# Another token block goes first through the final sums of a mixture-of-experts layer

## The chip, the cores and the metric

The kernel runs on one core of one Trainium2 chip. The metric is the device time of one execution in microseconds (us). Three executions of the kernel before took 1310.18, 1311.14 and 1313.49 us; their median is 1311.14 us.

The profile's short names are PE (TensorE, matrix multiplication), PEld (its weight loads), DVE (VectorE), ACT (ScalarE), POOL (GpSimd) and SP (SyncE, which here only issues DMAs). L473 is line 473 of the kernel before. In the changed kernel the same code stands one to eight lines lower.

## The reference

The layer takes 512 tokens of 1024 numbers. A mixing part gives the residual stream `x`; a mixture of 32 experts, of which each token uses four, is added to it; and a last norm is taken of every token:

```python
    x = x + jnp.concatenate([dn_out, pool_out], axis=-1) @ w_out[l]
    x = x + _moe(_rmsnorm(x, ffn_norm_w[l]), w_router[l], b_router[l],
                 w_gate_up[l], b_gate_up[l], w_down[l], b_down[l])
return _rmsnorm(x, final_norm_w)
```

Here `_rmsnorm(x, w)` is `x * rsqrt(mean(x*x) + 1e-6) * w` over the 1024 numbers of a token. The change touches only the last addition and the last norm.

## The kernel before

The kernel has one instruction list for each engine, written out by hand, and semaphores between them. Nothing reorders the lists, so the order of the code is the order of the work on each engine, and DMAs that SP issues go into one queue in the order of issue.

By far the longest part is a loop over blocks of 32 token assignments of one expert. PE multiplies with weights that SP streams into a ring of buffers; ACT scales the block's result (L851) and POOL writes it to DRAM with an indirect DMA (L604). POOL computes the row numbers of the next block (L600) only when its last indirect DMA has landed, and ACT waits for those row numbers before it writes the result for POOL. The results of all experts but the last one go to `pair_rows`, four rows for each token. The last expert's blocks are added in DRAM straight to `x1_rows`, which holds the residual stream.

After the loop come the final sums. The 512 tokens are four blocks of 128 (`TB` is 4), numbered 0 to 3:

- SP loads the four pair rows of each token, 2 MB for each block (L467), as soon as the other experts' results are in DRAM. It loads the norm's weights (L470), and when the last indirect DMA has landed, the residual rows, 512 KB for each block (L473). Each set is issued in the order 0, 1, 2, 3.
- DVE adds the four pair rows of blocks 0, 1 and 2 (L1421, three additions a block), and then the residual rows to them (L1424).
- PE does both for block 3: sixteen matmuls with an identity matrix add its pair rows in PSUM (L1998), and four more add its residual rows (L2002). The sum stays in PSUM as `summed_last`. These wait for `y_in[3]` and `x_in[3]`, the semaphores of block 3's loads.
- For each block ACT squares the sum and adds up over a token (L871, with a read of the accumulator), then takes a root (L873).
- For each block DVE takes the reciprocal of that root (L1428) and scales the block by it and by the norm's weights (L1429). SP stores the block when it is scaled (L476).

Four semaphores tie this together: `fin_sum` counts DVE's residual sums, `side_ps` tells that PE's sum is complete, `fin_rt` counts ACT's roots, and `fin_o` counts DVE's scaled blocks. In the kernel before, ACT, the scaling and the stores all take the blocks in the order 0, 1, 2, 3, and DVE finishes its three residual sums ahead of its first scaling.

Of the kernel before, what the change touches and what calls it, by code (L numbers as in the profile page):

```python
# [16 lines left out]
ALU, ACT, AX = mybir.AluOpType, mybir.ActivationFunctionType, mybir.AxisListType  # L17
# [4 lines left out]
TB = T // P  # L22
# [31 lines left out]
def moe_block(nc, x, attn_norm_w, w_in, conv_w, a_log, dt_bias, dn_norm_w, pool_w, pool_scale, w_out,  # L54
# [3 lines left out]
    with ctx:  # L58
        def sb(name, shape, dt=F32):
            return ctx.enter_context(nc.sbuf_tensor(name, shape, dt))  # L60

        def sem(name):
            return ctx.enter_context(nc.semaphore(name))
# [44 lines left out]
        xs = ring[:, X0 * UNIT:HOMES * UNIT].rearrange("p (b d) -> p b d", b=TB)  # L108
# [43 lines left out]
        sm = sb("sm", [P, 48])  # L152
# [15 lines left out]
        fnw = shared[:, 0:D]  # L168
# [52 lines left out]
        summed_last = ps[:, 4:6, :].rearrange("p a b -> p (a b)")  # L221
# [22 lines left out]
        def bc(v, n, at):  # L244

            return v.unsqueeze(at).to_broadcast([*v.shape[:at], n, *v.shape[at:]])
# [3 lines left out]
        par_in, wba_in, bc_in, pool_router_in, fnw_in, wout_in, braw_in = [sem(n) for n in (  # L250
            "par_in", "wba_in", "bc_in", "pool_router_in", "fnw_in", "wout_in", "braw_in")]
# [32 lines left out]
        fin_sum, fin_sq, fin_rt, fin_o, stored, act_step = [sem(n) for n in (  # L284
            "fin_sum", "fin_sq", "fin_rt", "fin_o", "stored", "act_step")]
# [5 lines left out]
        def chain(eng, s, start=0):  # L291

            n = [0]

            def link(ins):
                n[0] += 1
                ins.then_inc(s, 1)
                eng.wait_ge(s, start + n[0])
            link.n = n
            return link  # L300
# [11 lines left out]
        def slot_of(j, u):  # L312

            return (NU * j + u) % RING, (NU * j + u) // RING
# [6 lines left out]
        x1_quarters = x1_rows.rearrange("t (q c) -> (t q) c", q=Q)  # L321
        zeros = cat[:, 2048:2048 + D]
        pairs_in = ring[:, 4 * UNIT:12 * UNIT].rearrange("p (b c) -> p b c", b=TB)
        assert all(not 4 <= slot_of(E - 1, u)[0] < 12 for u in range(NU))

        halves = [slice(0, D // 2), slice(D // 2, D)]
# [26 lines left out]
        def _(sp):  # L353
# [109 lines left out]

            sp.wait_ge(scattered, others * 16)
            sp.wait_ge(late_out, 2 * 16)
            for b in range(TB):
                sp.dma_start(pairs_in[:, b], y_pairs[b * P:(b + 1) * P, :]).then_inc(y_in[b], 16)  # L467
            blocks = sp.value_load(tab[0:1, E:E + 1], min_val=E, max_val=MAXB)
            sp.wait_ge(w_used, blocks * NU)
            sp.dma_start(fnw, final_norm_w.rearrange("(a n) -> a n", a=1).to_broadcast([P, D])).then_inc(fnw_in, 16)  # L470
            sp.wait_ge(scattered, sp.value_load(looped[0:1, 2:3], min_val=E - 2, max_val=MAXB) * 16)
            for b in range(TB):
                sp.dma_start(xs[:, b, :], x1_rows[b * P:(b + 1) * P, :]).then_inc(x_in[b], 16)  # L473
            for b in range(TB):
                sp.wait_ge(fin_o, b + 1)
                sp.dma_start(out[0, b * P:(b + 1) * P, :], xs[:, b, :]).then_inc(stored, 16)  # L476
            sp.wait_ge(stored, 16 * (TB + 2))

# [158 lines left out]
        def _(act):  # L637
            A = nc.scalar.activation
            link = chain(act, act_step)
# [223 lines left out]
            with act.Fori(first, blocks) as g:  # L863
                activate(g)
            link(A(sm[:, 36:37], epsc[:, 0:1], ACT.Sqrt))
            for b in range(TB):
                if b < TB - 1:
                    act.wait_ge(fin_sum, b + 1)
                else:
                    act.wait_ge(side_ps, 4 + 2 + NU - NGU + 1)  # L870
                A(pairs_in[:, b, D:2 * D], xs[:, b, :] if b < TB - 1 else summed_last, ACT.Square, accum_out=sm[:, 28 + b:29 + b]).then_inc(fin_sq, 1)  # L871
                act.wait_ge(fin_sq, b + 1)
                A(sm[:, 32 + b:33 + b], sm[:, 28 + b:29 + b], ACT.Sqrt, scale=1.0 / D, bias=epsc[:, 0:1]).then_inc(fin_rt, 1)  # L873


# [1 line left out]
        def _(dve):  # L877
            V = nc.vector
            link = chain(dve, dve_step)

            def step(ins, s, count):

                ins.then_inc(s, 1)
                dve.wait_ge(s, count)
# [14 lines left out]
                                        op0=ALU.mult, op1=ALU.subtract))  # L899
# [23 lines left out]
            for k in range(KD):  # L923
                dve.wait_ge(xt_ps, k + 1)
                V.scalar_tensor_tensor(out=hT[:, k, :], in0=bank(k if k < KD - 1 else 2), scalar=pcol[:, NANW + k:NANW + k + 1],  # L925
                                       in1=rrow, op0=ALU.mult, op1=ALU.mult).then_inc(ht_ok, 1)
# [41 lines left out]
            def chunked(v):  # L968
# [21 lines left out]
                                        in1=bc(gt[:, 4, 0:2], NCH, 1), op0=ALU.mult, op1=ALU.mult), g_ok, 1)  # L990
# [296 lines left out]
            def swiglu_half(g, half, done, b, to=actT, told=actt_ok, by=1):  # L1287
# [4 lines left out]
                else:  # L1292
# [34 lines left out]
                                        op0=ALU.mult, op1=ALU.add))  # L1327
# [23 lines left out]
                                      op0=ALU.mult, op1=ALU.add))  # L1351
# [9 lines left out]
                                        op0=ALU.mult, op1=ALU.add))  # L1361
# [56 lines left out]
            for b in range(TB - 1):  # L1418
                dve.wait_ge(y_in[b], 16)
                for k in range(1, TOPK):  # L1420
                    link(V.tensor_tensor(pairs_in[:, b, 0:D], pairs_in[:, b, 0:D], pairs_in[:, b, k * D:(k + 1) * D], ALU.add))  # L1421
            for b in range(TB - 1):
                dve.wait_ge(x_in[b], 32)
                step(V.tensor_tensor(xs[:, b, :], xs[:, b, :], pairs_in[:, b, 0:D], ALU.add), fin_sum, b + 1)  # L1424
            dve.wait_ge(fnw_in, 32)
            for b in range(TB):
                dve.wait_ge(fin_rt, b + 1)
                link(V.reciprocal(sm[:, 44 + b:45 + b], sm[:, 32 + b:33 + b]))  # L1428
                V.scalar_tensor_tensor(out=xs[:, b, :], in0=xs[:, b, :] if b < TB - 1 else summed_last, scalar=sm[:, 44 + b:45 + b], in1=fnw, op0=ALU.mult,  # L1429
                                       op1=ALU.mult).then_inc(fin_o, 1)  # L1430


        @block.tensor
# [596 lines left out]
```

## Time and profile before

| what | before |
|---|---|
| median of three executions | 1311.14 us |
| the profiled execution | 1310.26 us, of which the span from first to last instruction is 1308.5 us |
| PE busy | 1263.3 us, 97% of the span |
| DVE busy | 515.7 us, 39% |
| ACT busy | 190.9 us, 15% |
| POOL busy | 162.7 us, 12% |
| DMA | 455.73 MB, 348 GB/s over the span |
| from the last matmul of the expert loop to the span's end | 25.0 us (1283.55 to 1308.5) |

The profiled execution is one of the quicker ones: it lies 0.9 us under the median of the three. Times within it count from the first instruction. The shares are averages over the whole span, in which the expert loop takes nearly all; the change lies in the last 25 us, so those are to be read by themselves.

### The profile page before, as it was taken

Reading aid. Unit: us, or ns where it says so; the run is one execution under the profiler, and the core shown is the slowest. Engines: PE = TensorE matmul, PEld = TensorE weight load, DVE = VectorE, ACT = ScalarE, POOL = GpSimd, SP = SyncE. Lnnn points to the kernel's source line nnn. Section 1 sums busy time; section 2 is a strip of 40 time slices with the busy share of each in tenths; the row PEclk is TensorE's granted clock in tenths of the full one; section 3 lists DMA queues with packets and bytes.
Section 4 is the critical chain, followed back from the end, with each engine's and each line's share of the span. In section 5 each row is a group of like instructions: output and inputs, shape, how many; then the busy total and the mean of one; then the engine's idle time right before and its main releaser. Section 6 shows DMA issues by size and latency. Waiting matters only on the chain.

```text
span 1308.5 us, 52719 instructions
## 1 busy us (share of the span) xinstructions
PE 1263.3 (97%) x21836; PEld 744.7 (57%) x21837; DVE 515.7 (39%) x1734; ACT 190.9 (15%) x439; POOL 162.7 (12%) x267
## 2 busy tenths in 40 slices
PE   8999999999999999999999999999999999989885
PEld 4545655445565665665665665656656656645452
DVE  5554223347343343343343333333433433423237
ACT  3431123332000000100100010000000000000002
POOL 4100430122111011011011011011011010100111
PEclk9999999999999999999999999999999999999999
DMA  7453131509999999999999999999999999999997
GB/s 237 140 188 129 34 133 48 222 33 372 416 402 415 421 414 422 415 421 416 420 417 421 413 421 415 421 410 421 416 417 422 417 420 416 420 421 421 421 424 277
DMA packets 80504, 455.73 MB, mean 348 GB/s; under 512 B 11057, under 2 KB 23018, under 8 KB 30730
## 3 DMA queue, kind: packets, MB, share of 16 engines
q1 hardware_dynamic: 76400, 445.69, 83.6%
q0 software_dynamic: 3888, 8.40, 1.8%
q8 instruction: 86, 1.41, 0.4%
q14 instruction: 24, 0.20, 0.0%
q10 hardware_dynamic: 106, 0.04, 0.0%
HBM read 432.53 MB, written 23.27 MB: 348 GB/s over the span
## 4 chain that ended last, share of the span: by engine, by line
DMA 52%; PE 43%; DVE 2%; issue 1%; ACT 1%; SPq 0%; DVEq 0%; POOL 0%; POOLq 0%; ACTq 0%
DMA ring<-in_w_gate_up_dram 32%; DMA ring<-in_w_down_dram 18%; PE ps L1900 12%; PE ps L1476 11%; PE ps L1952 6%; PE ps L1496 4%; PE ps L1866 2%; PE ps L1537 2%; DMA x_rows_dram<-cat,rowi 1%; PE ps L1530 1%; PE ps L1932 1%; DMA ring<-x_rows_dram 0%; PE ps L1892 0%; DVE ring L1429 0%; PE ps L1622 0%
## 5 line engine op out<-in xcount | busy, mean ns | idle before, releaser
L1900 PE MATMUL ps<-ring,cat 128*32 128x256 f32 x9856 | 550.1, 380 | 5.0 <-DMA ring<-in_w_gate_up_dram 4.9
L1900 PEld LDWEIGHTS ps<-ring,cat 128*32 128x32 f32 x9856 | 303.4, 110 | 221.7 <-DMA ring<-in_w_gate_up_dram 7.4
L1952 PE MATMUL ps<-ring,cat 128*32 128x256 f32 x4800 | 278.0, 382 | 12.7 <-DMA ring<-in_w_down_dram 12.4
L1952 PEld LDWEIGHTS ps<-ring,cat 128*32 128x32 f32 x4800 | 143.0, 110 | 118.2 <-issue 10.9
L1476 PE MATMUL ps<-hbuf,ring 128*128 128x512 f32 x320 | 146.0, 601 | 1.7 <-DVE hbuf L925 1.7
L1270 DVE TENSOR_REDUCE wslot<-ps 128x2 f32<-128x6 f32 x75 | 12.4, 165 | 320.0 <-ACT cat L851 318.5
L604 POOL DMA_INDIRECT pair_rows_dram<-cat,rowi x73 | 72.8, 997 | 436.9 <-ACT cat L851 436.9
L843 ACT ACTIVATE cat<-cat 128x128 f32<-128x128 f32 x154 | 47.6, 309 | 521.0 <-DVE cat L1294 521.0
L1866 PE MATMUL ps<-hbuf,cat 128*32 128x256 bf16 x2432 | 104.9, 273 | 1.1 <-DVE cat L1394 1.1
L1476 PEld LDWEIGHTS ps<-hbuf,ring 128*128 128x128 f32 x320 | 58.2, 190 | 67.2 <-issue 65.6
L1294 DVE TENSOR_SCALAR cat<-ps 128x128 f32<-128x128 f32 x154 | 44.8, 291 | 127.6 <-PE ps L1900 127.5
L851 ACT ACTIVATE cat<-ps,wslot 128x256 f32<-128x256 f32 x75 | 35.6, 474 | 369.7 <-PE ps L1952 363.5
L1866 PE MATMUL ps<-aux,cat 128*32 128x256 bf16 x1216 | 87.0, 273 | 0.0
L1866 PEld LDWEIGHTS ps<-hbuf,cat 128*32 128x32 bf16 x2432 | 66.6, 97 | 17.0 <-DVE cat L1394 1.6
L600 POOL TENSOR_TENSOR rowi<-rowj,qcol 128x1 int32<-128x1 int32 x75 | 15.7, 209 | 419.5 <-DMA pair_rows_dram<-cat,rowi 391.5
L1389 DVE COPY selu<-E 96x32 bf16 x75 | 13.3, 177 | 124.4 <-issue 124.4
L1496 PE MATMUL ps<-ring,cat 128*128 128x512 f32 x128 | 58.5, 600 | 2.3 <-DVE ring L1185 1.4
L1394 DVE TENSOR_TENSOR cat<-iotaf,rank 128x512 bf16 x75 | 51.9, 692 | 12.0 <-DVE gie L1390 12.0
L1302 DVE STREAM_TRANSPOSE cat<-cat 128x128 f32<-128x128 f32 x154 | 48.0, 312 | 5.3
L1298 DVE SCALAR_TENSOR_TENSOR cat<-cat 128x128 f32<-128x128 f32 x154 | 45.0, 292 | 5.3
L1301 DVE TENSOR_TENSOR cat<-cat 128x128 f32<-128x128 f32 x154 | 45.0, 292 | 5.2
L1295 DVE TENSOR_SCALAR cat<-ps 128x128 f32<-128x128 f32 x154 | 43.2, 281 | 0.0
(363 smaller groups left out, 817.3 us busy)
## 6 DMA issues: line engine op xcount, KB each, us to landing
ring<-in_w_gate_up_dram SPq DMA_DIRECT2D x256, 1024.0 KB, 10.0
ring<-in_w_down_dram SPq DMA_DIRECT2D x128, 1024.0 KB, 9.9
ring<-in_w_in_dram SPq DMA_DIRECT2D x10, 1024.0 KB, 6.3
pair_rows_dram<-cat SPq DMA_DIRECT2D x4, 2048.0 KB, 11.0
ring<-pair_rows_dram SPq DMA_DIRECT2D x4, 2048.0 KB, 19.8
ring<-in_w_out_dram SPq DMA_DIRECT2D x1, 4096.0 KB, 14.1
ring<-in_x_dram SPq DMA_DIRECT2D x4, 512.0 KB, 5.0
x_rows_dram<-ring SPq DMA_DIRECT2D x2, 1024.0 KB, 11.0
```

The source lines that it names most:

```text
L604: G.indirect_dma_start(out=into, out_offset=bass.IndirectOffsetOnAxis(ap=rowi[:, 0:1], axis=0), in_=ys, in_offset=None, bounds_check=limit ...
L843: A(sg[:, half], gc[:, half], ACT.Sigmoid, scale=ALPHA).then_inc(sg_ok, 1)
L1294: V.tensor_scalar(chunked_half(gc[:, half]), in_order(ps[:, b, 0:P]), LIMIT, None, ALU.min).then_inc(gc_ok, 1)
L1298: step(V.scalar_tensor_tensor(out=uc[:, half], in0=uc[:, half], scalar=1.0, in1=gc[:, half], op0=ALU.add, op1=ALU.mult), uc_step, n * 2 + 2)
L1301: step(V.tensor_tensor(act_[:, half], uc[:, half], sg[:, half], ALU.mult), act_ok, n + 1)
L1302: V.transpose(to[:, half], act_[:, half]).then_inc(told, by)
L1394: step(V.tensor_tensor(hot[:, :, :, :], slots, mine, ALU.is_equal), hot_ok, count)
L1476: last = mm(bank(m % 2), win[:, piece % 3, k, m % 2 * P:(m % 2 + 1) * P], hT[:, k, :], start=k == 0, stop=k == KD - 1)
L1496: last = mm(bank(n % 2), catT[:, k, b * P:(b + 1) * P], wout[:, k, 512 * half:512 * (half + 1)], start=i == 0, stop=i == KD - 1)
L1866: last = mm(ps[SLOTS * q:SLOTS * (q + 1), 2, 0:QD].rearrange("p (j i) -> p j i", i=SLOTS), hot[:, b, 0, :], rows, start=b == 0 and n == 0, ...
L1900: last = mm(ps[SLOTS * q:SLOTS * (q + 1), banks[half], 0:2 * P].rearrange("p (s m r) -> p s m r", s=2, m=2), x[:, SLOTS * u:SLOTS * (u + 1 ...
L1952: last = mm(ps[SLOTS * q:SLOTS * (q + 1), 1, 0:QD], actT[:, c // 4, SLOTS * (c % 4):SLOTS * (c % 4 + 1)], w[:, i, q * QD:(q + 1) * QD], st ...
```

## The change

A tuple `FINAL`, which is (3, 0, 1, 2), takes the place of the order 0, 1, 2, 3 in the pair loads, the residual loads, ACT's squares and roots, the scaling and the stores. DVE's list is also woven anew: after its residual sums of blocks 0 and 1 it scales one block each. Which engine sums which block, the number of instructions and all shapes stay as they are.

```diff
+        FINAL = (TB - 1, *range(TB - 1))
...
-            for b in range(TB):
+            for b in FINAL:
                 sp.dma_start(pairs_in[:, b], y_pairs[b * P:(b + 1) * P, :]).then_inc(y_in[b], 16)
...
-            for b in range(TB):
+            for b in FINAL:
                 sp.dma_start(xs[:, b, :], x1_rows[b * P:(b + 1) * P, :]).then_inc(x_in[b], 16)
-            for b in range(TB):
-                sp.wait_ge(fin_o, b + 1)
+            for n, b in enumerate(FINAL):
+                sp.wait_ge(fin_o, n + 1)
                 sp.dma_start(out[0, b * P:(b + 1) * P, :], xs[:, b, :]).then_inc(stored, 16)
...
-            for b in range(TB):
+            for n, b in enumerate(FINAL):
                 if b < TB - 1:
                     act.wait_ge(fin_sum, b + 1)
                 else:
                     act.wait_ge(side_ps, 4 + 2 + NU - NGU + 1)
                 A(pairs_in[:, b, D:2 * D], xs[:, b, :] if b < TB - 1 else summed_last, ACT.Square, accum_out=sm[:, 28 + b:29 + b]).then_inc(fin_sq, 1)
-                act.wait_ge(fin_sq, b + 1)
+                act.wait_ge(fin_sq, n + 1)
...
+            def scaled(n):
+
+                b = FINAL[n]
+                dve.wait_ge(fin_rt, n + 1)
+                link(V.reciprocal(sm[:, 44 + b:45 + b], sm[:, 32 + b:33 + b]))
+                V.scalar_tensor_tensor(out=xs[:, b, :], in0=xs[:, b, :] if b < TB - 1 else summed_last, scalar=sm[:, 44 + b:45 + b], in1=fnw, op0=ALU.mult,
+                                       op1=ALU.mult).then_inc(fin_o, 1)
+
+            dve.wait_ge(fnw_in, 32)
             for b in range(TB - 1):
                 dve.wait_ge(x_in[b], 32)
                 step(V.tensor_tensor(xs[:, b, :], xs[:, b, :], pairs_in[:, b, 0:D], ALU.add), fin_sum, b + 1)
-            dve.wait_ge(fnw_in, 32)
-            for b in range(TB):
-                dve.wait_ge(fin_rt, b + 1)
...
+                if b < TB - 2:
+                    scaled(b)
+            for n in range(TB - 2, TB):
+                scaled(n)
```

The end of DVE's list before, from the first residual sum on; `x_in0` to `x_in2` are the residual loads of blocks 0 to 2, and the row that reads `ps` scales block 3:

```order
L1424 TENSOR_TENSOR ring<-ring 128x1024 [waits x_in0,dve_step]
L1424 TENSOR_TENSOR ring<-ring 128x1024 [waits x_in1,fin_sum]
L1424 TENSOR_TENSOR ring<-ring 128x1024 [waits x_in2,fin_sum]
L1428 RECIPROCAL sm<-sm 128x1 [waits fin_rt,fnw_in,fin_sum]
L1429 SCALAR_TENSOR_TENSOR ring<-ring,sm 128x1024 [waits dve_step]
L1428 RECIPROCAL sm<-sm 128x1 [waits fin_rt]
L1429 SCALAR_TENSOR_TENSOR ring<-ring,sm 128x1024 [waits dve_step]
L1428 RECIPROCAL sm<-sm 128x1 [waits fin_rt]
L1429 SCALAR_TENSOR_TENSOR ring<-ring,sm 128x1024 [waits dve_step]
L1428 RECIPROCAL sm<-sm 128x1 [waits fin_rt]
L1429 SCALAR_TENSOR_TENSOR ring<-ps,sm,ring 128x1024 [waits dve_step]
```

The same end of DVE's list after:

```order
L1434 TENSOR_TENSOR ring<-ring 128x1024 [waits x_in0,fnw_in,dve_step]
L1427 RECIPROCAL sm<-sm 128x1 [waits fin_rt,fin_sum]
L1428 SCALAR_TENSOR_TENSOR ring<-ps,sm,ring 128x1024 [waits dve_step]
L1434 TENSOR_TENSOR ring<-ring 128x1024 [waits x_in1]
L1427 RECIPROCAL sm<-sm 128x1 [waits fin_rt,fin_sum]
L1428 SCALAR_TENSOR_TENSOR ring<-ring,sm 128x1024 [waits dve_step]
L1434 TENSOR_TENSOR ring<-ring 128x1024 [waits x_in2]
L1427 RECIPROCAL sm<-sm 128x1 [waits fin_rt,fin_sum]
L1428 SCALAR_TENSOR_TENSOR ring<-ring,sm 128x1024 [waits dve_step]
L1427 RECIPROCAL sm<-sm 128x1 [waits fin_rt]
L1428 SCALAR_TENSOR_TENSOR ring<-ring,sm 128x1024 [waits dve_step]
```

The scaling of block 3 moved from the end to the second place; it now stands ahead of the residual sums of blocks 1 and 2, and the last pair of rows scales block 2.

ACT's list before, its last five rows, from the root of block 1 on:

```order
L873 ACTIVATE sm<-sm,epsc 128x1 [waits fin_sq]
L871 ACTIVATE ring,sm<-ring 128x1024 [waits fin_sum]
L873 ACTIVATE sm<-sm,epsc 128x1 [waits fin_sq]
L871 ACTIVATE ring,sm<-ps 128x1024 [waits side_ps]
L873 ACTIVATE sm<-sm,epsc 128x1 [waits fin_sq]
```

ACT's list after, the five rows from the table load for the roots on:

```order
L866 ACT_TABLE_LOAD
L866 ACTIVATE sm<-epsc 128x1
L872 ACTIVATE ring,sm<-ps 128x1024 [waits side_ps,act_step]
L874 ACTIVATE sm<-sm,epsc 128x1 [waits fin_sq]
L872 ACTIVATE ring,sm<-ring 128x1024 [waits fin_sum]
```

The square of block 3, which reads PSUM and waits for PE, moved from the last place to the first, and block 0's square now stands behind it.

## Rows read from the trace of the kernel before

**Rows 1.** The page's chain that ended last: share of the span by engine.

```profile
DMA 52%; PE 43%; DVE 2%; issue 1%; ACT 1%; SPq 0%; DVEq 0%; POOL 0%; POOLq 0%; ACTq 0%
```

**Rows 2.** Chain that ended last, from 1272 us: start us, us, what.

```profile
1272.19 11.39 DMA x_rows_dram<-cat,rowi
...
1283.97 1.24 POOL rowi L600
...
1286.61 4.68 DMA x_rows_dram<-cat,rowi
...
1291.67 0.43 SPq L473
...
1292.15 6.27 DMA ring<-x_rows_dram
...
1298.52 1.24 DVE ring L1424
...
1299.78 0.17 DVE sm L1428
...
1299.98 1.28 DVE ring L1429
...
1304.16 1.28 DVE ring L1429
```

**Rows 3.** Timeline from 1279 us: start us, us, instructions in order, [idle before].

```profile
1279.92 3.63 PE L1952 MATMUL ps<-ring,cat 128*32 128x256 f32 x64
1280.19 11.26 DVE L1421 TENSOR_TENSOR ring<-ring 128x1024 f32<-128x1024 f32 x9
...
1288.97 8.70 PE L1998 MATMUL ps<-ring,cat 128*128 128x512 f32 x16 [5.42 <-DMA ring<-pair_rows_dram]
...
1290.80 0.34 PEld L1998 LDWEIGHTS ps<-ring,cat 128*128 128x128 f32 x1 [0.52 <-issue]
...
1291.66 0.34 PEld L1998 LDWEIGHTS ps<-ring,cat 128*128 128x128 f32 x1 [0.52 <-issue]
...
1294.08 0.19 PEld L1998 LDWEIGHTS ps<-ring,cat 128*128 128x128 f32 x1 [0.24 <-issue]
1294.50 0.19 PEld L1998 LDWEIGHTS ps<-ring,cat 128*128 128x128 f32 x1 [0.24 <-issue]
...
1299.72 1.98 PE L2002 MATMUL ps<-ring,cat 128*128 128x512 f32 x4 [2.05 <-DMA ring<-x_rows_dram]
...
1301.74 1.02 ACT L871 ACTIVATE ring<-ps 128x1024 f32<-128x1024 f32 x1 [0.48 <-PE ps L2002]
...
1302.89 0.29 ACT L873 ACTIVATE sm<-sm,epsc 128x1 f32<-128x1 f32 x1
```

**Rows 4.** From issue to landing, us: L467's four; its second; L473's four; its second; L476's.

```profile
DMA to landing us min/median/max: 12.7/19.8/26.7
...
ring<-pair_rows_dram SPq DMA_DIRECT2D x1, 2048.0 KB, 17.3
...
DMA to landing us min/median/max: 3.2/5.2/7.1
...
ring<-x_rows_dram SPq DMA_DIRECT2D x1, 512.0 KB, 4.2
...
DMA to landing us min/median/max: 2.6/2.6/2.7
```

**Rows 5.** POOL: L600 from 200 to 1250 us (ns min/median/max), then L604's last two.

```profile
L600 POOL TENSOR_TENSOR rowi<-rowj,qcol x73: 177/179/353, 329.8 to 1248.0; 128x1 int32<-128x1 int32 x73
...
1272.19 1.62 POOL L604 DMA_INDIRECT x_rows_dram<-cat,rowi  x1 [10.35 <-ACT cat L851]
...
1286.61 2.52 POOL L604 DMA_INDIRECT x_rows_dram<-cat,rowi  x1 [1.41 <-ACT cat L851]
```

**Rows 6.** Stretches: busy us (count) of PE, PEld, DVE, ACT, POOL; PEclk; DMA.

```profile
1288.70:1288.80 0.10, 0.00 (x0) 0.00 (x0) 0.10 (x1) 0.00 (x0) 0.10 (x1) 0.90 0.41 164
...
1305.75:1306.00 0.25, 0.00 (x0) 0.00 (x0) 0.00 (x0) 0.00 (x0) 0.00 (x0) 0.69 0.92 377
```

More of the change, by code:

```diff
@@ L1424, in _ @@
                 step(V.tensor_tensor(xs[:, b, :], xs[:, b, :], pairs_in[:, b, 0:D], ALU.add), fin_sum, b + 1)
-            dve.wait_ge(fnw_in, 32)
-            for b in range(TB):
-                dve.wait_ge(fin_rt, b + 1)
-                link(V.reciprocal(sm[:, 44 + b:45 + b], sm[:, 32 + b:33 + b]))
-                V.scalar_tensor_tensor(out=xs[:, b, :], in0=xs[:, b, :] if b < TB - 1 else summed_last, scalar=sm[:, 44 + b:45 + b], in1=fnw, op0=ALU.mult,
-                                       op1=ALU.mult).then_inc(fin_o, 1)
+                if b < TB - 2:
+                    scaled(b)
+            for n in range(TB - 2, TB):
+                scaled(n)
         @block.tensor
```

## The prediction

> **What bounds the kernel now.** I read the chain that ended last first, then the timeline of the last 30 us. Over the whole span the chain is DMA and PE, that is, the expert loop [rows 1], which the change leaves alone. In the last 25 us the chain is another one [rows 2]. An indirect DMA lands at 1272.19 + 11.39 = 1283.58; POOL computes the next row numbers (1283.97, 1.24 us); then come ACT's copy and POOL's last indirect DMA (1286.61, landed 4.68 later, at 1291.29); only now may SP issue the residual loads. The third of them, block 2's, lands 6.27 after 1292.15, at 1298.42. DVE adds it (1298.52, 1.24 us) and then scales four blocks without a pause, one every 1.39 us, until 1304.16 + 1.28 = 1305.44. The last store takes 2.6 us [rows 4], and the span ends at 1308.5, 3.06 after DVE's last instruction.
>
> Block 3, the block that PE sums, is on no critical path at the end. PE waits until 1288.97 for its pair rows, is through with them at 1297.67, and adds the residual rows from 1299.72 to 1301.70 [rows 3]. ACT's root is there at 1302.89 + 0.29 = 1303.18, and DVE is still scaling until 1304.04. So 0.9 us of slack is all that an earlier block 3 has to work with; DVE's queue, and the loads that feed it, set the end.
>
> **Pair loads.** They go in one queue, in whatever order. The fourth landed just before 1288.97; with issues 0.43 us apart [rows 2] and 12.7, 17.3, 22.3 (from the median, 2 x 19.8 - 17.3) and 26.7 us to landing [rows 4], the four landed at about 1273.6, 1278.5, 1284.0 and 1288.9. After the change these are blocks 3, 0, 1, 2. PE is in the expert loop until 1283.55 [rows 3], so its sixteen matmuls start there and not at 1288.97. Their weight loads are 0.86 us apart at the start and 0.42 us later (1290.80 to 1291.66, 1294.08 to 1294.50) [rows 3]. At the quick pace sixteen take 16 x 0.43 = 6.9 us, to about 1290.5, 7 us earlier than before. DVE's nine additions began at 1280.19 and ran without a gap [rows 3], 1.25 us each. Now block 0's three still begin then; block 1's wait a moment for 1284.0; block 2's wait from 1287.8 for 1288.9 and end at 1292.6 instead of 1291.45. That 1.2 us costs nothing: block 0's residual rows come later.
>
> **Residual loads.** If they are issued as before, they land at 1291.3 + 3.2 = 1294.5, at 1291.67 + 4.2 = 1295.87, at 1298.42 and at about 1299.7 (the fourth is what PE waited for until 1299.72) [rows 2 to 4]. The first two are now blocks 3 and 0. DVE's first residual sum moves from the first landing to the second.
>
> **The tail, step by step,** with the rows' durations. PE adds block 3's residual rows from 1294.54, 1.98 us, to 1296.52. ACT needs 1303.18 - 1301.70 = 1.48 us more: root at 1298.00. Meanwhile DVE does block 0's sum (1295.95 to 1297.18) and then stands still for 0.87 us, because its next instruction is block 3's reciprocal, which waits for that root; behind it in DVE's queue stand the sums of blocks 1 and 2, which before the change ran ahead of every scaling. From 1298.05: reciprocal and scaling to 1299.53 (0.20 + 1.28), block 1's sum to 1300.78 (1.25), block 0's scaling to 1302.29, block 2's sum to 1303.54, block 1's scaling to 1305.05. Block 2's root is ready 1.58 us after its sum, at 1305.12, so its scaling runs to 1306.60. Blocks 1 and 2 landed at 1298.42 and 1299.7 and are not waited for. That is 1306.60 against 1305.44: **1.16 us later**. The reason in one line: before, two of the three sums were done in the time in which DVE had to wait for the third load anyway; now only one is.
>
> **POOL.** One thing may give some of this back. The computing of row numbers took 179 ns at the median of 73 times, 353 at most [rows 5], but 1.24 us the last time [rows 2], beside DVE's gapless additions; and the last indirect DMA took 2.52 us on POOL, the one before it, with DVE mostly idle, 1.62 [rows 5]. Both are in the chain that releases the residual loads. Now DVE has two gaps: one of about 0.1 us at 1283.95, just where the row numbers begin (1283.97), and one of 1.1 us from 1287.8, within the indirect DMA. The relief lies between 0 and (1.24 - 0.18) + (2.52 - 1.62) = 1.96 us. If POOL gets the first gap, 1.06 are won, but its DMA is then set up beside block 1's additions, as slow as before. If DVE starts first, the first 1.06 are lost and the second gap saves up to 0.9. Either way nearest to 0.8; the last pair and weight loads are then still in flight, so I take 0.7.
>
> The Trainium skill (SBUF — State Buffer, Who interferes with whom) has it that a DVE instruction with two inputs in SBUF and a GpSimd instruction that reads SBUF shut each other out, whoever starts first keeping the ports to its end. The row numbers' 1.24 us, which end with DVE's addition, agree. The same section infers that setting up an indirect DMA is not slowed by such additions; then the second gap is worth nothing, and the sum would be between +0.1 and +1.2. The 2.52 against 1.62 us here speak against that.
>
> **Sum.** +1.16 - 0.7 = +0.5 us. The profiled execution took 1310.26, 1.76 more than its span; it would become 1310.7. The runs' median lies 0.9 above it, so I forecast a median of 1311.14 + 0.5 = 1311.6.
>
> **Rivals.**
> - *Slower: PE's clock.* PE now pauses between the pair sums (1290.5) and block 3's residual rows (1293.8 to 1294.5), for 3.3 to 4.0 us. The granted clock fell to half at 1288.78, 5.2 us after the last matmul, and again at 1305.84, 4.1 us after it [rows 3, 6]; a pause of 2.05 us did not do it (four matmuls in 1.98 us behind it). The new pause lies between. If it falls, the four matmuls go at 0.86 and not 0.43 us apart, 1.7 us longer, and since DVE waits for block 3's root, all of it arrives at the end: +2.2, that is 1313.3. It decides when the pause reaches the shorter of the two falls. It would need the pair sums at half clock too (16 x 0.43 = 6.9 more, of which some 3.5 fit into the pause) to come above +4; but PE comes straight from the loop at full clock.
> - *Faster: POOL is freed entirely.* Both reliefs, 1.96 us: +1.16 - 1.96 = -0.8, 1310.3. For it: DVE's two gaps are where POOL needs them. Against it: an earlier indirect DMA moves out of the second gap.
> - *No relief on POOL,* if DVE takes up block 1 first and the set-up is as slow as before: +1.2, 1312.3.
> - *The change does not do what it says:* PE starts its pair sums late, for its code or a wait I do not see. Until about 1287.5 that only fills the pause and costs nothing; so it changes the time little.
>
> **How the numbers follow.** Chances: the forecast, with a relief of 0.3 to 1.2 us, 0.55 (its own range is 1311.1 to 1312.0); no relief 0.18; POOL freed entirely 0.12; PE's clock 0.11; something larger than all these 0.04. The cases reach from -0.8 to +2.2, 1310.3 to 1313.3, and the three runs shown lie 3.3 us apart, so that a median of a few moves by about 1 us: 1309.2 to 1314.4. What a measurement of this kernel can tell from no change is 0.3%, 3.9 us. No case reaches that far down, since everything before 1283 stays and a relief beyond 1.96 has no row; 1 to 2 in 100 for faster, 5 for slower.
>
> **What would show it.** Right: PE's pair sums begin within 1 us of the loop's last matmul; the first matmul on residual rows starts right after the first residual load lands; DVE has an idle stretch of 0.5 to 1.2 us between block 0's sum and the first reciprocal, which ACT ends; the last scaling ends 0 to 1.2 us later than 1305.44, counted from 1283.58, when the last indirect DMA but one landed. POOL's two durations, 1.24 and 2.52 us, give the relief. Wrong: DVE idle behind its second scaling, for the loads of block 1 or 2; the four matmuls taking over 3 us; the residual loads issued later than 7.7 us after that landing, as they were before; or a shift of more than 2 us that begins ahead of the last expert.

## The result, and the profile after

The changed kernel took 1314.12 us at the median of 22 executions (1312.29 to 1317.58), the kernel before 1311.95 us at the median of 22 (1308.54 to 1314.56). The ratio is 1.0021, with a 95% interval of 1.0015 to 1.0028: 2.0 to 3.7 us slower. That is less than 0.3%, but it is no longer noise. I had forecast +0.5 us.

The profiled execution of after took 1316.46 us, span 1314.7 us, against 1310.26 and 1308.5 before. These 6.2 us are not all the change's. The last indirect DMA but one, ahead of which the change alters only the order of the pair loads, landed at 1286.23 instead of 1283.58, 2.7 us later. Such differences come between executions of one kernel: in two more traces of after it landed at 1283.6 and 1282.5, in one more of before at 1285.1. The tail behind it is 3.6 us longer. In after, L1434 is DVE's residual sum, L1427 and L1428 are its reciprocal and scaling, L2006 and L2010 PE's pair and residual sums, L872 and L874 ACT's square and root. The chain of the tail (start us, us, what):

```profile
1275.14 11.09 DMA x_rows_dram<-cat,rowi
...
1286.63 0.19 POOL rowi L601
...
1288.22 5.91 DMA x_rows_dram<-cat,rowi
...
1294.15 3.91 DMA ring<-x_rows_dram
...
1298.10 3.65 PE ps L2010 x4
...
1301.83 1.12 ACT ring L872 x2
...
1302.98 0.30 ACT sm L874
...
1303.38 0.18 DVE sm L1427
```

Beside [rows 2]: POOL's row numbers now take 0.19 and not 1.24 us, yet the last indirect DMA lands 7.9 us behind the one before it, as it did before (7.7). Then the chain no longer runs through block 2's load to DVE, but through block 3's load, PE and ACT; block 3's root is what DVE waits for. The timeline of PE in after (start us, us, line, [idle before]) and that of DVE:

```profile
1285.86 7.13 PE L2006 MATMUL ps<-ring,cat 128*128 128x512 f32 x16
1298.10 3.63 PE L2010 MATMUL ps<-ring,cat 128*128 128x512 f32 x4 [5.11 <-DMA ring<-x_rows_dram]
```

```profile
1299.43 1.22 DVE L1434 TENSOR_TENSOR ring<-ring 128x1024 f32<-128x1024 f32 x1 [2.96 <-DMA ring<-x_rows_dram]
1303.38 0.16 DVE L1427 RECIPROCAL sm<-sm 128x1 f32<-128x1 f32 x1 [2.72 <-ACT sm L874]
1303.58 1.28 DVE L1428 SCALAR_TENSOR_TENSOR ring<-ps,sm,ring 128x1024 f32<-128x1024 f32 x1
1304.78 1.22 DVE L1434 TENSOR_TENSOR ring<-ring 128x1024 f32<-128x1024 f32 x1
...
1310.39 1.28 DVE L1428 SCALAR_TENSOR_TENSOR ring<-ring,sm 128x1024 f32<-128x1024 f32 x1
```

PE's pair sums start right behind the loop and take 7.1 us, as forecast. Then PE pauses 5.1 us, and its four residual matmuls take 3.63 us where they took 1.98 [rows 3]. DVE makes block 0's sum and then stands for 2.7 us, with the residual sums of blocks 1 and 2 queued behind the reciprocal that waits. The stretches show the clock (behind the busy times: PEclk, the granted share of the full clock; DMA share; GB/s). It falls to half at 1298.3, 0.2 us after PE has taken up work again:

```profile
1297.50:1298.00 0.50, 0.00 (x0) 0.00 (x0) 0.00 (x0) 0.00 (x0) 0.00 (x0) 1.00 1.07 410
1298.00:1299.00 1.00, 0.90 (x2) 0.38 (x3) 0.00 (x0) 0.00 (x0) 0.00 (x0) 0.65 0.96 365
1299.00:1300.00 1.00, 1.00 (x3) 0.48 (x2) 0.57 (x1) 0.00 (x0) 0.00 (x0) 0.50 1.01 406
```

### The profile page after: what moved, and what is told of

It is laid out like the page before. It is cut to its first block, busy times and chain, and to the rows that moved or that the text cites. A ratio compares the mean times of both kernels' runs of the same rounds, so it can differ in the third digit from the quotient of the medians.

```text
span 1314.7 us, 52720 instructions
## 1 busy us (share of the span) xinstructions
PE 1261.5 (96%) x21837; PEld 745.4 (57%) x21837; DVE 515.2 (39%) x1734; ACT 190.9 (15%) x439; POOL 161.4 (12%) x267
## 4 chain that ended last, share of the span: by engine, by line
PE 51%; DMA 44%; DVE 2%; issue 1%; ACT 0%; SPq 0%; DVEq 0%; ACTq 0%; POOLq 0%; POOL 0%
DMA ring<-in_w_gate_up_dram 27%; PE ps L1908 16%; DMA ring<-in_w_down_dram 16%; PE ps L1484 11%; PE ps L1960 8%; PE ps L1504 4%; PE ps L1874 3%; PE ps L1545 2%; DMA x_rows_dram<-cat,rowi 1%; PE ps L1900 1%; PE ps L1538 1%; PE ps L1940 1%; PE ps L1951 0%; DMA ring<-in_ffn_norm_w_dram 0%; PE ps L1883 0%
## 5 line engine op out<-in xcount | busy, mean ns | idle before, releaser
L1960 PE MATMUL ps<-ring,cat 128*32 128x256 f32 x4800 | 277.2, 380 | 14.4 <-DMA ring<-in_w_down_dram 13.7
L1874 PEld LDWEIGHTS ps<-hbuf,cat 128*32 128x32 bf16 x2432 | 67.0, 97 | 16.9 <-DVE cat L1395 1.6
L1390 DVE COPY selu<-E 96x32 bf16 x75 | 13.3, 178 | 124.3 <-issue 124.3
```

The lines of the kernel that those rows point to most:

```text
L1874: last = mm(ps[SLOTS * q:SLOTS * (q + 1), 2, 0:QD].rearrange("p (j i) -> p j i", i=SLOTS), hot[:, b, 0, :], rows, start=b == 0 and n == 0, ...
L1960: last = mm(ps[SLOTS * q:SLOTS * (q + 1), 1, 0:QD], actT[:, c // 4, SLOTS * (c % 4):SLOTS * (c % 4 + 1)], w[:, i, q * QD:(q + 1) * QD], st ...
```

## The experiments

Executions of one kernel lie 3 to 6 us apart, mostly from what comes before the tail, so each trace is read by its tail. G is the time from the landing of the last indirect DMA but one to that of the last; S is the time from there to the end of DVE's last scaling. T in the expectations is G + S. "Pause" is PE's idle time ahead of the four residual matmuls, "four" their time, "first load" the time from issue to landing of the residual load that is issued first. All in us. The expectations count from landings read to 0.1, so that some of their S differ by 0.1 from this table.

| run | pause | four | first load | G | S | time against before (95%) |
|---|---|---|---|---|---|---|
| before | 2.1 | 1.98 | 3.2 | 7.7 | 14.2 | |
| after | 5.1 | 3.63 | 3.9 | 7.9 | 17.5 | 1.0021 (1.0015 to 1.0028) |
| e1 after again | 5.1 | 3.57 | 3.6 | 8.3 | 17.1 | 1.0031 (1.0020 to 1.0042) |
| e2 PE kept busy, eight lines | none | 1.88 | 3.6 | 8.4 | 16.9 | 1.0029 (1.0020 to 1.0039) |
| e3 sums first | 5.3 | 3.78 | 3.6 | 8.6 | 14.9 | 1.0005 (0.9996 to 1.0014) |
| e4 pair loads only | 5.9 | 3.78 | 3.3 | 7.6 | 14.1 | 1.0013 (1.0004 to 1.0021) |
| e5 PE kept busy, four lines | 2.0 | 1.99 | 3.7 | 8.8 | 15.7 | 1.0025 (1.0015 to 1.0035) |
| e6 before again | 0.3 | 1.98 | 3.4 | 8.6 | 14.3 | 1.0006 (0.9997 to 1.0016) |
| e7 after, old pair order | none | 1.88 | 3.6 | 7.6 | 18.5 | 1.0050 (1.0035 to 1.0064) |
| e8 weave on before | 1.5 | 1.98 | 3.2 | 8.6 | 13.3 | 0.9999 (0.9990 to 1.0008) |
| e9 after, third | 5.5 | 3.46 | 3.8 | 8.8 | 17.3 | 1.0033 (1.0021 to 1.0045) |
| e10 e5 again | 2.0 | 3.27 | 3.7 | 8.7 | 17.0 | 1.0016 (1.0006 to 1.0026) |
| e11 e4 with e5's matmuls | 5.8 | 3.60 | 3.2 | 8.5 | 14.4 | 1.0011 (1.0001 to 1.0020) |
| e12 e8 again | 0.8 | 1.98 | 3.1 | 8.7 | 13.4 | 1.0000 (0.9991 to 1.0009) |

**e1 and e9: after, twice more.** No edit.

> The changed kernel once more, for a second trace of it. I count the tail T from the landing of the last indirect DMA but one (of the last expert) to the end of DVE's last scaling: 21.9 us in the trace of before, 25.4 in the first trace of after. Theory A (PE's clock falls in its pause before block 3's residual rows, and DVE's second instruction waits for block 3's root): the four residual matmuls take 3.6 us again and T is 25 to 25.5; if they take 2.0, T is 23.5 to 24. Theory B (the first residual load lands later because of the new order of loads, 3.9 us after issue and not 3.2): it takes 3.7 us or more again. Both could hold. Against before: +2 to +3 us.

> After for a third trace, beside e10 on the same chip. S is the time from the landing of the last indirect DMA to the end of the last scaling: 14.1 us (before), 14.3 (e6), 17.6 (after), 17.2 (e1). Theory A (the clock falls in PE's pause each time): S = 17.2 to 17.6, the four residual matmuls take 3.6 us. Rival (it falls in some executions only, and by chance in all the traces so far): S = 15.5 to 16 and 2.0 us. Time +2.5 to +3.5 us over before.

The clock fell in all three traces of after; S is 17.1 to 17.5, 3.1 us above the two traces of before on average. Theory A holds for the clock; what DVE's wait has to do with it is the question of e3. The times are 4.1 and 4.3 us over before, more than I expected, with intervals that begin at 2.6 and 2.8 us. Theory B holds in part. G is 7.6 to 8.8 whatever the order of the loads, so the order does not show there. The first residual load, however, took 3.6 to 3.9 us in all eight traces in which it is block 3's, and 3.1 to 3.4 us in all six in which it is block 0's. The order of the pair loads does not matter for this: e7 has the old one and 3.6 us, e4 and e11 have the new one and 3.3 and 3.2 us. So about 0.4 us here belongs to the change's new order of the residual loads. Why block 3's rows take longer when they go first is open.

**e6: before, once more.** No edit.

> The kernel before, for a second trace of it. T = 21.9; the last indirect DMA lands 7.7 us after the one before it; the first residual load takes 3.2 us. If these two come out at 8.2 and 3.6, as in the traces of after, their difference was that of executions and not the change's. Time as before.

G came out at 8.6, so for G the second case holds: my rows of before happened to show a short one. The first load took 3.4 us. POOL in e6 and then in e5 (start us, us, line):

```profile
1285.51 1.23 POOL L600 TENSOR_TENSOR rowi<-rowj,qcol 128x1 int32<-128x1 int32 x1 [9.58 <-DMA x_rows_dram<-cat,rowi]
1288.15 2.52 POOL L604 DMA_INDIRECT x_rows_dram<-cat,rowi  x1 [1.41 <-ACT cat L851]
```

```profile
1286.28 0.18 POOL L601 TENSOR_TENSOR rowi<-rowj,qcol 128x1 int32<-128x1 int32 x1 [9.54 <-DMA x_rows_dram<-cat,rowi]
1287.87 1.58 POOL L605 DMA_INDIRECT x_rows_dram<-cat,rowi  x1 [1.41 <-ACT cat L852]
```

The landings before these were at 1285.1 and 1285.9. So e5's POOL was through with the set-up 3.6 us after that landing, e6's 5.6 us after it, and both last DMAs landed 8.6 to 8.8 us after it. POOL was freed, just as I had thought it might be, and it was worth nothing. What G does go with is the pair loads: where the fourth of them landed 5.3 to 5.7 us after the last indirect DMA but one (before, e4, e7), G is 7.6 to 7.7; in the other eleven traces it landed 6.4 to 7.2 us after, and G is 7.9 to 8.8. In every trace the last indirect DMA lands 0.2 to 1.2 us behind the load of the norm's weights, which SP issues after the pair loads (in e5 at 1285.98, to landing 8.5 us; in before at 1283.62, 6.5 us). Both point to DMA engines that were not through earlier; no run takes those loads away, so it is the likeliest reading and not shown. It fits the Trainium skill (DMA: Bandwidth & Descriptors, Issuing engines are not separate DMA queues): DMAs of all issuing engines end up on the same 16 DMA engines and interleave there.

**e2, e5 and e10: PE kept at work in the pause.** The edit, with 8 in e2 and 4 in e5 and e10:

```diff
+            for _ in range(4):
+                mm(ps[:, 6, :], ident_late, pairs_in[:, TB - 1, 0:512], start=True, stop=True)
             pe.wait_ge(x_in[TB - 1], 32)
```

> After, with eight more matmuls of 128x512 into an unused PSUM bank between block 3's pair sums and its wait for the residual rows (8 x 0.43 = 3.4 us, inside the pause of 5.1 us). Their result is not used. Theory A: the clock stays at full, the four residual matmuls take 2.0 and not 3.6 us, T is 23.8, and the kernel is 1.6 us faster than after, 1.1 us slower than before. Rival (DVE's order alone costs all of it): T stays at 25.4 and the time equals after's.

A miss, since I had sized the edit wrongly: each line of code is two matmuls in the trace (L2009 below), so eight lines ran for 7.0 us, past the landing of block 3's rows (1293.5 + 3.6 = 1297.1). The four residual matmuls went at full clock, but 1.5 us late:

```profile
1291.71 7.03 PE L2009 MATMUL ps<-ring,cat 128*128 128x512 f32 x16
1298.58 1.88 PE L2012 MATMUL ps<-ring,cat 128*128 128x512 f32 x4
```

> After, with four more matmuls of 128x512 into an unused PSUM bank behind block 3's pair sums (their result is not used). The trace of e2 showed eight such lines of code as 7.0 us of work, not 3.4, so there they reached 1.5 us past the landing of the residual rows; four are 3.5 us, inside a pause of 5.1. Theory A (PE's clock): the pause left is 1.6 us, the clock stays at full, the four residual matmuls take 1.9 to 2.0 us and not 3.6; T (landing of the last indirect DMA but one to the end of the last scaling) is 23.8 and not 25.4, and the time is 1.6 us under after's. Rival (loads and DVE's order alone): T 25.4, time as after's.

In the trace theory A holds: four matmuls in 1.99 us, S = 15.7, 1.6 us under the mean of after's three. T is 24.5, not 23.8, because of G. The time, however, was not shorter than after's, so it was run again:

> e5 once more. Its trace had S = 15.7, 1.7 less than after's, but its times were no shorter than after's: what came before the last landing was longer. Theory A with that difference put down to the spread between executions and builds: S = 15.7 again, and now the time 1 to 2 us under e9's. Rival (the added matmuls delay something ahead of the last landing): S = 15.7, the last landing 8.7 us or more after the one before it, and a time not under e9's.

This trace shows why four lines are no sure remedy. PE's pause is 2.0 us as in e5, and the clock falls all the same, half a microsecond into the residual matmuls. The timeline and the stretches of e10:

```profile
1291.80 3.60 PE L2009 MATMUL ps<-ring,cat 128*128 128x512 f32 x8
1297.39 3.27 PE L2012 MATMUL ps<-ring,cat 128*128 128x512 f32 x4 [2.00 <-DMA ring<-x_rows_dram]
```

```profile
1297.50:1298.00 0.50, 0.50 (x2) 0.26 (x3) 0.00 (x0) 0.00 (x0) 0.00 (x0) 0.94 1.06 393
1298.00:1298.50 0.50, 0.50 (x2) 0.23 (x1) 0.00 (x0) 0.00 (x0) 0.00 (x0) 0.50 1.02 418
```

So the edit does not keep the clock up in every execution. S is 17.0 and not 15.7. The median of e10 lies 1.9 us under e9's on the same chip, as expected, but in the traces its tail is only 0.3 us shorter than e9's, so they do not show that the clock made this difference. Over both runs its 23 times have a mean of 1314.2 us, the 35 of after (with e1 and e9) one of 1314.8: a gain of the expected sign, but not clear of the spread. That the clock costs the tail 1.6 us is shown by the traces (e5 against after's three); by the times alone it is not.

**e3: DVE's sums first.** All else as in after:

```diff
-                if b < TB - 2:
-                    scaled(b)
-            for n in range(TB - 2, TB):
+            for n in range(TB):
                 scaled(n)
```

> After, but DVE makes its three residual sums first, as before the change, and then scales blocks 3, 0, 1, 2. Loads, ACT and stores keep the new order. Theory A with DVE's queue: block 3's root, late or not, is then waited for behind work that DVE has anyway; the end goes 2.6 us down to T = 22.8, 1 us slower than before. Theory B alone (late loads): the end is set by the last residual load, T = 24.5 or more.

This is the experiment that settles most. The clock fell here too (four in 3.78 us), but S is 14.9, 2.4 us under the mean of after's three, and the time is back within noise of before. The times alone tell e3 from after: its interval and that of e1, taken on the same chip, do not meet. DVE now does its sums in the time in which block 3's root is late (timeline of DVE in e3):

```profile
1297.79 1.23 DVE L1434 TENSOR_TENSOR ring<-ring 128x1024 f32<-128x1024 f32 x1 [3.16 <-DMA ring<-x_rows_dram]
1299.43 2.48 DVE L1434 TENSOR_TENSOR ring<-ring 128x1024 f32<-128x1024 f32 x2 [0.42 <-DMA ring<-x_rows_dram]
1301.95 0.16 DVE L1427 RECIPROCAL sm<-sm 128x1 f32<-128x1 f32 x1
```

The reciprocal has no idle time ahead of it, where after had 2.72 us. T was 23.4 and not 22.8, again because of G.

**e4 and e11: only the pair loads reordered, without and with e5's matmuls.** The edit of e4 on the kernel before:

```diff
-            for b in range(TB):
+            for b in (TB - 1, *range(TB - 1)):
                 sp.dma_start(pairs_in[:, b], y_pairs[b * P:(b + 1) * P, :]).then_inc(y_in[b], 16)
```

> Before, with only the pair loads in the new order (block 3 first), everything else as before. My prediction's step: PE's sixteen matmuls start 5 us earlier and nothing else moves, T = 21.9, time as before within 0.5 us. Theory B in the form that the new order of the pair loads itself delays the last indirect DMA or the residual loads: T = 22.8, +0.9 us.

> e4 (before with only the pair loads in the new order) with the four matmuls of e5 behind the pair sums. In e4's trace PE paused 5.9 us, its four residual matmuls took 3.8 us, and DVE waited 0.95 us for block 3's root ahead of the last scaling. Theory A: the clock stays up, they take 2.0, DVE does not wait, S = 13.2 to 14.2, and the time is 1 us under e4's (+1.4 over before). Rival: e4's time had another cause and stays.

In e4 T was 21.7, as my step had it, but the price of the early pair sums is seen in the trace: the pause is 5.9 us, the clock falls, and block 3, which had 0.9 us of slack, is late (DVE in e4):

```profile
1303.59 1.28 DVE L1429 SCALAR_TENSOR_TENSOR ring<-ring,sm 128x1024 f32<-128x1024 f32 x1
1305.82 0.17 DVE L1428 RECIPROCAL sm<-sm 128x1 f32<-128x1 f32 x1 [0.95 <-ACT sm L873]
```

e11 did not test what it was to test: block 3's residual rows come fourth there, and behind the added matmuls there were still 5.8 us of pause. Both kernels were 1.1 to 1.3 per mille (1.4 to 1.7 us) slower than before, where I had expected e4 within 0.5 us, while their S is at most 0.2 us above the mean of before's two. More than 1 us of their time, by the ratios as they stand, is unexplained. The kernel before, built and run again as e6, came out 0.6 per mille (-0.3 to 1.6) above the others of its kind; a part may be that.

**e7: after, with the pair loads in the old order.**

```diff
-            for b in FINAL:
+            for b in range(TB):
                 sp.dma_start(pairs_in[:, b], y_pairs[b * P:(b + 1) * P, :]).then_inc(y_in[b], 16)
```

> After, with the pair loads in the order 0, 1, 2, 3 again; residual loads, ACT, DVE and stores keep the new order. PE then makes block 3's pair sums 5 us later, in part at half clock, and is through with them only about 1.5 us after block 3's residual rows land, but has no pause: the four residual matmuls take 2.0 us. Theory A: what is won on the clock is lost on the late pair sums, T = 25.5 to 26. Theory C (the new order of the pair loads itself delays the last indirect DMA, 8.2 and not 7.7 us, and the first residual load): both fall back to the values of before and T = 24.8 to 25.2.

T is 26.2, a little over theory A's figure, and the time is 3.5 to 6.4 per mille over before's. PE comes late with the pair sums, and DVE stands for 4.0 us (PE's timeline of e7, then DVE's):

```profile
1290.03 8.66 PE L2006 MATMUL ps<-ring,cat 128*128 128x512 f32 x16 [5.45 <-DMA ring<-pair_rows_dram]
1298.53 1.88 PE L2010 MATMUL ps<-ring,cat 128*128 128x512 f32 x4
```

```profile
1302.05 0.16 DVE L1427 RECIPROCAL sm<-sm 128x1 f32<-128x1 f32 x1 [4.02 <-ACT sm L874]
```

Theory C fails: G did come out short, at 7.6, but it is as short in e4 with the new pair order and 8.6 to 8.7 in e6, e8 and e12 with the old one, and the first load did not fall back. The pair loads' new order is the part of the change that pays, 1.2 us of S, once the rest is there.

**e8 and e12: another weaving, on the kernel before.** Old order everywhere; DVE scales block 0 between its sums of blocks 1 and 2:

```diff
-            for b in range(TB - 1):
...
-            dve.wait_ge(fnw_in, 32)
-            for b in range(TB):
+            def scaled(b):
                 dve.wait_ge(fin_rt, b + 1)
...
+            dve.wait_ge(fnw_in, 32)
+            for b in range(TB - 1):
+                dve.wait_ge(x_in[b], 32)
+                step(V.tensor_tensor(xs[:, b, :], xs[:, b, :], pairs_in[:, b, 0:D], ALU.add), fin_sum, b + 1)
+                if b == TB - 3:
+                    scaled(0)
+            for b in range(1, TB):
+                scaled(b)
```

> Before, with all loads, ACT and stores in the old order, but DVE scales block 0 between its residual sums of blocks 1 and 2, in the 1.4 us in which it waits for block 2's rows. By the rows of before: scaling of block 0 from 1297.45, block 2's sum from 1298.9, the other scalings without a pause, end 0.75 us earlier; T = 21.1, time -0.7 us. Rival: block 2's rows land without that pause in most executions (e4's third load landed 2.7 us after its first, 0.2 us of waiting), so nothing is won: T = 21.9.

> e8 once more, the version with the shortest tail so far (S = 13.3; 0.8 under before), to see if its time is shorter than before's. Theory: S = 13.2 to 13.5, time -0.4 to -0.9 us. Rival: the wait for block 2's rows is short in most executions, S = 14.

In the edit `b == TB - 3` is block 1. S is 13.3 and 13.4, the shortest tails of all, 0.8 us under before, as worked out (T of e8 is 21.9 and not 21.1, because of G). The scaling of block 0 now lies in the wait for block 2's rows (DVE in e12, where L1431 is the residual sum, L1424 and L1425 are reciprocal and scaling):

```profile
1295.36 2.59 DVE L1431 TENSOR_TENSOR ring<-ring 128x1024 f32<-128x1024 f32 x2 [4.03 <-DMA ring<-x_rows_dram]
1298.26 0.16 DVE L1424 RECIPROCAL sm<-sm 128x1 f32<-128x1 f32 x1 [0.31 <-ACT sm L873]
1298.46 1.28 DVE L1425 SCALAR_TENSOR_TENSOR ring<-ring,sm 128x1024 f32<-128x1024 f32 x1
1299.66 1.22 DVE L1431 TENSOR_TENSOR ring<-ring 128x1024 f32<-128x1024 f32 x1
```

In the times this cannot be told from before (0.9999 and 1.0000, each to within 0.9 per mille). It is the best version by the trace, not one proved faster.

## Why the prediction was wrong

- *PE's clock: the step that failed.* I had the pause at 3.3 to 4.0 us, and so between what had and what had not let the clock fall, and gave the fall 0.11. The pause was 5.1 to 5.5 us in after's three traces, and the clock fell in each. The price was right: 1.7 us worked out, 1.5 to 1.65 measured. That rival's total was 1313.3; the measured median is 1314.1. The pause was longer for two reasons: the residual loads were not issued sooner (7.9 to 8.8 us after the landing before, where I had reckoned with 7.7 less the relief), and the first took 3.6 to 3.9 us and not 3.2. The condition was wrong too, that the clock falls only when the pause reaches 4.1 us: in e10 it fell behind 2.0 us. Rows of the trace of before that the prediction does not use said as much; they stand below.
- *POOL's relief of 0.7 us: not there.* POOL's computing of the row numbers did get shorter, 1.24 to 0.18 us, in DVE's gap. I counted that at the end of the chain without asking what the indirect DMA itself would then wait for. G does not get shorter with the relief (e5 against e6); the loads still in flight are the likeliest reason. G also varies from 7.6 to 8.8 whatever the edit, and I had one trace of it, one of the shortest.
- *DVE's new weave and the later first sum, +1.16 us: right.* e5, where the clock held, has S = 15.7 against 14.2 and 14.3 before, +1.45. The rest over 1.16, 0.3 us, is about what block 3's rows, going first, took longer to land (3.7 us against 3.2 and 3.4).
- *DVE standing for block 3's root, 0.87 us: right in place, too short.* It was 2.5 to 2.7 us, and 1.03 in e5, where the clock held. e3 shows that this wait is what brings the clock's loss to the end: with the sums ahead of it DVE did not wait at all behind the same slow matmuls.
- *Pair loads: right.* PE started within 0.5 us of the loop's end, and DVE's 1.2 us later pair sums cost nothing.

The rows of before that bear on the clock's condition are from the expert loop, where PE waits for weights. The timeline of PE, then the stretches:

```profile
1235.79 1.07 PE L1952 MATMUL ps<-ring,cat 128*32 128x256 f32 x16 [1.22 <-DMA ring<-in_w_down_dram]
1238.19 1.93 PE L1952 MATMUL ps<-ring,cat 128*32 128x256 f32 x16 [1.33 <-DMA ring<-in_w_down_dram]
```

```profile
1236.50:1237.00 0.50, 0.36 (x8) 0.00 (x0) 0.00 (x0) 0.00 (x0) 0.00 (x0) 1.00 1.03 426
1237.00:1238.00 1.00, 0.00 (x0) 0.00 (x0) 0.00 (x0) 0.00 (x0) 0.00 (x0) 0.79 1.02 426
1238.00:1239.00 1.00, 0.81 (x8) 0.40 (x12) 0.00 (x0) 0.00 (x0) 0.00 (x0) 0.50 1.00 418
```

Here the clock fell to half within the second of two pauses of 1.2 and 1.3 us. Two pauses of 1.33 us each around 1206 left it at full. So the length of one pause did not decide, and my 0.11 for this rival rested on too few rows.

Put together, +1.16 - 0.7 became +1.5 (order, with the slower first load) + 1.6 (clock) + 0 (POOL) = +3.1 us of S in the traces; the times say +2.0 to +3.7.

## What to carry to other kernels

Where an engine's queue holds work that is ready, an instruction that must wait for another engine should not stand ahead of it: behind the sums DVE did not wait at all (e3), in front of them it stood for 2.5 to 2.7 us (the three traces of after). Starting an engine's work earlier can open a pause behind it, and for TensorE a pause has a price of its own; reckon the pause by the latest landing that the traces allow, not by the one in hand, and look through the whole trace for the shortest pause behind which the clock has fallen. A shorter step in a chain is worth only what the next step can use, so ask what that one waits for.

## What the runs showed of the hardware

- The granted clock fell to half in all six traces with a PE pause of 5.1 to 5.9 us ahead of the residual matmuls, and in e10 after a pause of only 2.0 us, 0.5 us after PE had taken up work. In e5 and in the kernel before a pause of the same length left it at full. In the loop of before it fell at 1237.6 within the second of two pauses of 1.2 and 1.3 us, and two pauses of 1.33 us each around 1206 left it at full. In the six traces it fell between 3.5 us ahead of PE's first residual matmul and 0.3 us behind it, and it stayed down for all or nearly all of the four.
- An accumulating indirect DMA whose set-up ended 1 to 2 us earlier landed no earlier while large loads were in flight (G of 8.6 in e6 and 8.8 in e5).
- The first of the four residual loads took 3.6 to 3.9 us when it was block 3's (eight traces) and 3.1 to 3.4 us when it was block 0's (six), with the same size.
- The set-up took 1.58 us in e4, e5 and e9 beside DVE's additions, and 2.3 to 2.6 us in the other traces, with additions running there too, so the additions do not slow it each time. How the two happen to fall on each other may decide; no run is on that alone.
